# The last 24 dots with gathered rows of u moved among the first steps over v, and the weights scratch laid out by chunk

## The reference, cut to what matters

```python
def chunk(xc):                       # 128 tokens at a time, 4 such chunks of tokens
    q  = (xc @ wq).reshape(128, 8, 2, 128)
    s1, s2 = ...                     # scores against two sets of 128 keys, 8 heads
    v1, i1 = lax.top_k(s1, 16);  v2, i2 = lax.top_k(s2, 16)
    best, pos = lax.top_k(v1[..., :, None] + v2[..., None, :], 16)   # best 16 pairs
    eidx = i1 * 128 + i2             # 8 heads x 16 experts for every token
    g = jax.nn.softmax(best, axis=-1)
    a = jnp.einsum('chkd,cd->chk', u_tab[eidx], xc)                  # dots with rows of u
    wgt = jax.nn.gelu(a) * g
    return jnp.einsum('chk,chkd->cd', wgt, v_tab[eidx])              # sum of rows of v
```

## Time and profile before

| | |
|---|---|
| median of 3 runs | 2808.05 us (2804.38 to 2814.04) |
| the profiled execution | 2804.89 us, span 2803.1 us, mean granted PE clock 0.962 |
| PE busy | 2548.3 us, 91% of the span |
| DVE busy | 1560.5 us, 56% |
| ACT busy | 1045.3 us, 37% |
| POOL busy | 514.2 us, 18% |
| DMA | 606.02 MB, mean 216 GB/s; 81399 of 161265 packets under 2 KB |

### The profile page before, as it was taken

One profiled execution on the slowest core, in us unless ns is written; L12 is line 12 of the kernel. 1 busy time (PEld: TensorE's weight loads), 2 busy tenths in 40 slices (PEclk: granted clock), 3 DMA queues, 4 the chain that ended last, 5 costly groups with the idle time before them and its releaser, 6 DMA issues.

```text
span 2803.1 us, 31963 instructions
## 1 busy us (share of the span) xinstructions
PE 2548.3 (91%) x12808; PEld 1905.4 (68%) x12808; DVE 1560.5 (56%) x2856; ACT 1045.3 (37%) x1309; POOL 514.2 (18%) x427
## 2 busy tenths in 40 slices
PE   6998999578778899999899999988988999999997
PEld 4666676333233344777679999988888777777775
DVE  4524234421126656566527989899995444444444
ACT  4854432221004311674323333354553333333332
POOL 0100000000010000000000011234343265555550
PEclk9999999799888999999999999999999999999998
DMA  4433441699970000211033476698998888888892
GB/s 190 193 137 143 171 159 63 227 422 425 425 309 31 30 30 30 91 61 61 30 127 127 175 255 229 238 331 322 353 345 326 286 318 311 322 319 319 309 322 86
DMA packets 161265, 606.02 MB, mean 216 GB/s; under 512 B 15735, under 2 KB 81399, under 8 KB 128408
## 3 DMA queue, kind: packets, MB, share of 16 engines
q1 hardware_dynamic: 91104, 384.32, 36.8%
q0 software_dynamic: 44528, 154.69, 15.3%
q10 hardware_dynamic: 25480, 64.90, 6.1%
HBM read 533.08 MB, written 70.78 MB: 215 GB/s over the span
## 4 chain that ended last, share of the span: by engine, by line
PE 67%; DVE 16%; DMA 9%; issue 4%; ACT 3%; SPq 0%; POOL 0%; ACTq 0%; DVEq 0%; POOLq 0%
PE P L2680 6%; PE P L2681 6%; PE P L2682 6%; DVE window L592 5%; PE P L2560 4%; PE P L2562 4%; PE P L2561 4%; PE P L2216 3%; DMA ug<-in_ur,sparse 3%; PE P L2391 3%; DMA H<-in_w_up 2%; DVE part L592 2%; PE P L2631 2%; PE P L2019 2%; DVE ug L1385 2%
## 5 line engine op out<-in xcount | busy, mean ns | idle before, releaser
L592 DVE TENSOR_TENSOR part<-raw,part 128x2048 fp32r<-128x2048 f32 x136 | 311.4, 2290 | 414.8 <-ACT part L1869 414.7
L2560 PE MATMUL P<-hr,part 128*128 128x384 f32 (+1 forms) x1136 | 401.8, 354 | 42.9 <-DVE part L592 42.3
L2562 PE MATMUL P<-hr,part 128*128 128x384 f32 (+1 forms) x1136 | 395.7, 348 | 0.0
L2561 PE MATMUL P<-hr,part 128*128 128x384 f32 (+1 forms) x1136 | 395.6, 348 | 0.0
L2695 POOL DMA_INDIRECT ug<-in_ur,sparse x128 | 164.1, 1282 | 1130.6 <-DVE window L600 754.6
L1869 ACT ACTIVATE part<-raw 128x2048 fp32r<-128x2048 f32 x136 | 260.7, 1917 | 290.9 <-PE P L2682 268.7
L2680 PE MATMUL P<-part,ge 128*128 128x512 f32 x768 | 302.9, 394 | 0.7 <-issue 0.7
L2681 PE MATMUL P<-part,ge 128*128 128x512 f32 x768 | 299.5, 390 | 0.0
L2682 PE MATMUL P<-part,ge 128*128 128x512 f32 x768 | 299.0, 389 | 0.0
L2560 PEld LDWEIGHTS P<-hr,part 128*128 128x128 f32 x1136 | 218.1, 192 | 53.8 <-DVE part L592 47.9
L2561 PEld LDWEIGHTS P<-hr,part 128*128 128x128 f32 x1136 | 218.0, 192 | 4.9
(11 more groups left out here) (367 smaller groups left out, 4477.4 us busy)
## 6 DMA issues: line engine op xcount, KB each, us to landing
raw<-in_u SPq DMA_DIRECT2D x64, 1024.0 KB, 5.3
raw<-in_vd SPq DMA_DIRECT2D x64, 1024.0 KB, 7.8
W<-in_w_up SPq DMA_DIRECT2D x24, 2048.0 KB, 18.3
W<-in_w_in SPq DMA_DIRECT2D x18, 2048.0 KB, 8.6
W<-in_ada_w SPq DMA_DIRECT2D x12, 2048.0 KB, 7.8
a_scratch<-gt ACTq DMA_DIRECT2D x128, 192.0 KB, 4.0
w_scratch<-window ACTq DMA_DIRECT2D x12, 2048.0 KB, 11.6
wr<-w_scratch SPq DMA_DIRECT2D x32, 768.0 KB, 11.1
```

The lines of the kernel that those rows point to most:

```text
L592: return v.tensor_tensor(out=out_, in0=in0, in1=in1, op=op)
L2560: t.matmul(b, wh[:, k, js], HR[0][:, k, lo:S], start=k == 0, stop=False)
L2561: t.matmul(b, wh[:, k, js], HR[1][:, k, lo:S], start=False, stop=False)
L2562: ins = t.matmul(b, wl[:, k, js], HR[0][:, k, lo:S], start=False, stop=k == 7)
```

## The change

It has three parts.

1. The last 24 of the 128 dots leave `ORDER3`. The wg steps are interleaved with the other 67 at 0.7 per part. Six dots stand in each of the steps 0 to 3 over v, behind the parts of the next unit and ahead of "down".
2. "sw" leaves `ORDER3`: gelu and shares are in step 4 over v, the transpose behind "down" 4 (into bank 6 where it was bank 3), the copy behind "down" 5. The 64 sv and 4 wd entries start behind step 5, two or three per step, and end with step 30 where they ended with step 29. The wait for the copied weights at every "down" is gone.
3. `w_scratch` is laid out as 32 chunks of 128 partitions by 1536 values, where it was 12 blocks of 128 by 4096. The store of a block now writes 32 runs of 512 B per partition (4096 runs), where it wrote one of 16 KB. The load of a chunk reads one run of 6 KB per partition (128 runs), where it read 12 of 512 B (1536 runs).

```diff
-        Wd = nc.dram_tensor("w_scratch", [12, 128, 128 * 32], f32).ap()
+        Wd = nc.dram_tensor("w_scratch", [32, 128, 128 * 12], f32).ap()
...
-        wg_steps = interleave([("wg", x, i) for x in range(48) for i in range(2)], dots, 0.95) + dots + [("sw",)]
+        late = [dots.pop() for _ in range(24)][::-1]
+        wg_steps = interleave([("wg", x, i) for x in range(48) for i in range(2)], dots, 0.7) + dots
...
                 V_STEPS.append(("part", v_unit[n] + 2))
+                V_STEPS += [late.pop(0) for _ in range(6) if late]
+            if n == 4:
+                V_STEPS.append(("sw", 0))
             V_STEPS.append(("down", n))
-            for _ in range(3 if n % 4 == 0 else 2):
-                if turns and n < 31:
+            if n in (4, 5):
+                V_STEPS.append((("tw", "cw")[n - 4], 0))
+            for _ in range(3 if n % 3 else 2):
+                if turns and 5 <= n < 31:
                     V_STEPS.append(turns.pop(0))
...
-                v.tensor_copy(WT0, bank[3][:, 0:128]).then_inc(s["sw_v"], 1)
+
+            def turned_weights():
+                dve.wait_ge(s["hs_mm"], 3)
+                v.tensor_copy(WT0, bank[6][:, 0:128]).then_inc(s["sw_v"], 1)
...
-                    a.dma_start(Wd[tb], WS[tb % 2]).then_inc(s[f"ws{tb % 2}"], 16)
+                    a.dma_start(Wd.rearrange("c p (b i) -> b p c i", b=12)[tb], WS[tb % 2].rearrange("p (c i) -> p c i", c=32)).then_inc(s[f"ws{tb % 2}"], 16)
...
-                elif kind == "sw":
-                    pe.wait_ge(s["sc2_a"], 16)
-                    pe.wait_ge(s["sw_v"], 1)
-                    t.transpose(bank[3][:, 0:128], DOT, ident).then_inc(s["hs_mm"], 1)
...
+                if kind == "tw":
+                    pe.wait_ge(s["sw_v"], 1)
+                    t.transpose(bank[6][:, 0:128], DOT, ident).then_inc(s["hs_mm"], 1)
...
-                    pe.wait_ge(s["sw_v"], 2)
...
-                nc.sync.dma_start(WRB[n % 2].rearrange("p (b i) -> p b i", b=12),
-                                  Wd.rearrange("b p (c i) -> c p b i", c=32)[n]).then_inc(s[f"wq{n % 2}"], 16)
+                nc.sync.dma_start(WRB[n % 2], Wd[n]).then_inc(s[f"wq{n % 2}"], 16)
```

More of the change, by code:

```diff
@@ L568, in program @@
                 V_STEPS.append(("part", v_unit[n] + 2))
+                V_STEPS += [late.pop(0) for _ in range(6) if late]
+            if n == 4:
+                V_STEPS.append(("sw", 0))
             V_STEPS.append(("down", n))
-            for _ in range(3 if n % 4 == 0 else 2):
-                if turns and n < 31:
+            if n in (4, 5):
+                V_STEPS.append((("tw", "cw")[n - 4], 0))
+            for _ in range(3 if n % 3 else 2):
+                if turns and 5 <= n < 31:
                     V_STEPS.append(turns.pop(0))
-        assert not turns
+        assert not turns and not late
         ones_at = [i for i, x in enumerate(ORDER3) if x[0] == "wg"]
@@ L1453, in vector_program @@
                     row_dot(*i)
-                elif kind == "sw":
-                    row_weights()
-                elif kind == "wd":
-                    step_weights(*i)
             for kind, n in V_STEPS:
@@ L1461, in vector_program @@
                     weighted(n)
+                elif kind == "ud":
+                    row_dot(n)
+                elif kind == "sw":
+                    row_weights()
+                elif kind == "cw":
+                    turned_weights()
                 elif kind == "part":
@@ L1969, in scalar_program @@
                     first_parts(*i)
+            for kind, n in V_STEPS:
+                if kind == "up":
+                    first_parts(n)
                 elif kind == "sw":
@@ L1972, in scalar_program @@
                     a.activation(DOT, DOT, ACT.Gelu_apprx_tanh).then_inc(s["hs_a"], 1)
-            for kind, n in V_STEPS:
-                if kind == "up":
-                    first_parts(n)
                 elif kind == "part":
@@ L2640, in tensor_program @@
                     weights(*i)
-                elif kind == "sw":
-                    pe.wait_ge(s["sc2_a"], 16)
-                    pe.wait_ge(s["sw_v"], 1)
-                    t.transpose(bank[3][:, 0:128], DOT, ident).then_inc(s["hs_mm"], 1)
-                elif kind == "sv":
-                    row_sums(*i)
                 elif kind == "fx":
```

## The result

The changed kernel takes 2837.94 us (median of 4 runs, 2828.39 to 2839.29) where the kernel before took 2806.22 (4 runs, 2800.69 to 2814.04): a ratio of 1.0104, 95% interval 1.0070 to 1.0137. It is slower by 1%, above the forecast of 2799 and just above its range of 2768 to 2836; rival B, with a chance of 0.14, had said 2848.

What follows compares the result with a forecast made beforehand. DVE was taken to bound the wg steps, PE the steps over v. Against the profiled 2804.9 us, 30 + 5 - 5 - 18 - 3 = 9 us gained gives 2796; the runs' median is 3.2 higher: 2799 us, range 2768 to 2836.

Steps and rivals of the forecast that it cites:

- rival B: wg steps: 4096 runs hold ACT's queue, decisive from about 7 us; at 11.6 costs 54 us: 2848, slower; chance 0.14.
- The dots taken from the wg steps: wg steps: 24 dots fewer on DVE, 27.5 us of its work; stretch falls to 290, gain 30 us (15 to 37).
- Between: Between wg steps and steps over v: "sw" and the burst of 16 gathers go, gain 5 us (3 to 8).
- ACT's queue: wg steps: ACT's next store stands about 4 us behind each store of weights, twelve times; loss 5 us (0 to 54).
- Steps 0 to 3: Steps over v: six dots take 11.5 us, the fifth waiting for its gather, so PE waits; loss 18 us (3 to 45).
- Step 4 on: Steps over v: the burst of 16 gathers delays a unit of v at the end of step 3; loss 3 us (0 to 8).
- The load on the DMA engines: wg steps: load falls from 291 to about 276 us, under DVE's time; over v by 3% of the share; no term.

Runs made afterwards that it cites:

- e1: Changed kernel with the weights scratch in its old layout, so only the dots' order is new against the kernel before: 2784.85 us, ratio 0.9918.
- e12: The dot order of e10 with the weights scratch in its old layout (16 KB stores, reads in 512 B runs): 2777.39 us, ratio 0.9888.
- e9: e8 with eight gather buffers instead of four for the 24 dots among the steps over v: 2773.60 us, ratio 0.9879.
- e8: Changed kernel with each store of weights cut into four pieces of 1024 runs, issued by ACT behind the next four groups: 2784.09 us, ratio 0.9926.
- e3: Changed kernel with the stores of weights issued by SP instead of ACT, the same 4096 runs: 2788.94 us, ratio 0.9934.
- e4: Changed kernel with scratch laid out by pairs of chunks: stores of 2048 runs of 1 KB, loads in 512 B runs: 2789.41 us, ratio 0.9937.
- e10: e8 with four dots to a step over steps 0 to 5, sw, tw and cw two steps later, three sv per step from step 7: 2768.53 us.
- e11: e8 with both the eight gather buffers of e9 and the four dots to a step of e10: 2772.07 us, ratio 0.9877.
- e2: Kernel before with only the new layout of the weights scratch, its order of dots kept: 2837.23 us, ratio 1.0108.
- e7: e8 with three of each step's six dots ahead of the low part of the next step's first unit, three behind: 2789.77 us, ratio 0.9930.

## Why the prediction was wrong, step by step

- **The dots taken from the wg steps** (forecast 30, ends 37 and 15): right. Without the hold the stage takes 274.2 us instead of 307.8, 33.6 less (e1). DVE is still the bound, busy 272.0 of 274.4 us; 26.0 us of work left it, where 27.5 were forecast. The 8 us that the forecast left for PE and DVE to wait for each other were not needed, hence the 3.6 more.
- **Between** (5, ends 3 and 8): 5.5 in e1 and 6.3 in e12, where nothing is held; 1.2 in after, where the last hold falls into this stretch.
- **ACT's queue** (5 us, ends 0 and 54): this step failed. After against e1, the wg steps lose 51.1 us and the stretch between 4.3: 55. The mechanism was named, but the term was sized near its lower end, for three reasons. First, the hold. The forecast had the queue free 7 us after the issue of a store of weights, by the median of the earlier trace rows (1536 runs in 2.6 us). Measured, the issue behind ends 7.4 to 13.3 us after it (2010.61 to 2023.90 is the longest), 10.5 in the mean of twelve. The issues behind are held for 87.7 - 13 x 0.33 = 83 us in all. The earlier trace rows has an issue of 5.9 us beside its median of 2.05, and the forecast took the median. Second, the store behind was then held for about 4 us, against some 4 us of cover, and that left nearly nothing. With 10.5 the same sum gives 12 x (10.5 - 3.1 - 4) = 41, and PE waits 41.1 for line 1938. Third, ACT's idle half was counted on besides. It is of no use behind a blocked queue: line 1938 stands between PE and its two banks every 5.6 us. The clock was no part of the term; it cost 14.4 us. So the upper end of 54 met the 55 by luck: it had the queue held until the store has landed, 11.6 us, but in after the stores land after 12.8 us at the least and the queue is held 10.5, and it had nothing for the clock. Rival B had the mechanism, and the hold from which it decides, about 7 us from the store's issue (3.1 and 4 of cover), was passed by all twelve.
- **Steps 0 to 3** (18): the stage grew by 16.1, with DVE's waits as described; the reason (the late gathers, not DVE's work) is shown by e9. The parts are off and make up for each other: PE waits 11.9 us instead of 16, and the rest, mostly the lower clock, is 4 instead of 2. The half microsecond that the forecast put behind each wait was nearly 3 us behind the wait of 5.0.
- **Step 4 on** (3): nothing in after, where PE is busy without a gap from 2294 us on.
- **The load on the DMA engines** (no term): right for the wg steps (e8 stands at a share of 0.98). What reading in 6 KB runs gives to the gathers of v was counted as nothing. In before PE waits for no gather of v, in e1 for 8.6 us, in after, with 6 KB reads, for none; so the new layout probably gives something once the gathers of v stand closer.

Without the failed term the sum comes near: 2804.9 - 30 - 5 + 18 + 3 = 2791. The profiled executions of e3 and e8, in which ACT is held little or not at all, took 2791.3 and 2783.6 us, and that of e4, held for at most 5.0 us at a time, 2788.4.

The Trainium skill (DMA: Bandwidth & Descriptors, section Issuing engines are not separate DMA queues) says that the time of a sequencer to start a DMA is usually small beside the DMA itself. For the store of 4096 runs it is 0.38 us by its own row, but its successor's 10.2 is over half of the store's landing of 16.2 (the median of the twelve); the measurement decides. The same skill (Perfetto Trace Analysis, section What "DMA-bound" means) says that when an issuing engine's track is solid with DMA slices, these slices are the writing of descriptors and not the movement of data. The runs here show that the hold goes with the issuing queue (e3) and that the long slice stands at the DMA behind the large one. Whether it is the writing of descriptors they don't show.

## What to carry to other kernels

Before a store is cut into short runs, count its runs and look at what its queue issues next: here thousands of runs cost microseconds not in their own row but in the next one, on an engine that may be half idle and still be the bound. Put such a store on a queue that runs ahead, or in pieces between the engine's other work. When a term has ends as far apart as 0 and 54 us and the trace has a row that already shows the effect at a third of the size, take the far end as likely, look at the longest of that row and not only its median, and don't subtract a cover from it that was never measured. Work that is moved beside spare time gains only as much as the buffers of its inputs allow for one step.

## What the runs showed of the hardware

- The issue behind a DMA of many runs: 128 runs of 16 KB, nothing (334 ns at most, e1); 1536 runs (reads), 2.05 us by the median and 5.9 at most; 1024 runs of 512 B among other work, up to 1.2 us (e8) and 1.3 (e10); two such DMAs one behind the other, 6.1 us at the second (e8), or 8.3 and 9.1 at the issue behind both (e9, e11); 2048 of 1 KB, up to 5.0 (e4); 4096 of 512 B, 4.3 to 10.2 (after), up to 10.6 (e2). The same number of runs gives holds of very different length, so more than the count enters; whether the queue waits for descriptors to be written or for room that the transfers free was not told apart.
- A gather's issue on POOL takes 0.94 to 3.05 us for the same shape; in e7's timeline:

```profile
2163.49 3.05 POOL L2715 DMA_INDIRECT ug<-in_ur,sparse  x1 [0.30 <-issue]
2166.85 0.94 POOL L2715 DMA_INDIRECT ug<-in_ur,sparse  x1 [0.31 <-issue]
```

- Reads of 6 KB instead of 512 B runs bring other loads in sooner: units of v landed in 4.8 us by the median in after against 7.9 in the earlier trace rows, though POOL was busier with gathers, 323 us of 520 against 295.
